# Hybrid decoder block: activation sums and low halves moved from GpSimd to VectorE, eight weight units stored split

## The reference, cut to what matters

```python
mod = silu(c) @ w_ada + b_ada; shift, scale, gate = split(mod, 3)
h = rms_norm(x, norm_g) * (1 + scale) + shift          # (4096, 1024)
proj = h @ w_in                                        # (4096, 3592)
u, z_pool, q, k, v, o, z_mlstm, gates = columns of proj # 512 each, gates 8
pool_out = causal_pool_mixer(u) * silu(z_pool)         # windows 2, 4, 8, 16
q, k = silu(causal_depthwise_conv([q, k]))             # 4 taps
hm = mlstm_chunkwise(q, k, v, ig, log_sigmoid(fg))     # 4 heads of 128, chunks of 128 positions
mlstm_out = rms_norm_per_head(hm) * sigmoid(o) * silu(z_mlstm)
x = x + gate * ([pool_out, mlstm_out] @ w_out)
return rms_norm(x, final_g)
```

## Time and profile before

| What | Value |
| --- | --- |
| Runs, us | 1890.22, 1891.05, 1901.94 |
| Median, us | 1891.05 |
| Profiled execution, us | 1895.02 |
| Its span, first to last instruction, us | 1893.2 |
| Mean granted TensorE clock in it | 0.982 |
| DMA traffic, MB | 368.89 |

### The profile page before, as it was taken

How to read it: one execution, slowest core, us unless ns; L and a number is a source line. 1 busy time by engine, 2 the same in 40 slices (tenths; PEclk the granted TensorE clock), 3 DMA queues, 4 the chain that set the end, 5 groups by cost and what they waited for, 6 DMA issues and landing times.

```text
span 1893.2 us, 25429 instructions
## 1 busy us (share of the span) xinstructions
PE 1759.9 (93%) x8921; PEld 1484.7 (78%) x8921; DVE 1275.2 (67%) x2421; ACT 729.4 (39%) x1692; POOL 633.3 (33%) x491
## 2 busy tenths in 40 slices
PE   6989999989998999988999899998999989998898
PEld 6878879768897788867888678976789768897786
DVE  7786684857748586476855668476684866738583
ACT  4444342443425343343334434244242443424321
POOL 0145235430345204542155402634026430355200
PEclk9999999999999999999999999999999999999999
DMA  9998955468564774657755686446955469554762
GB/s 340 321 330 279 264 148 201 128 175 253 146 212 123 202 249 120 220 131 215 212 154 184 156 244 176 179 134 157 286 149 184 131 166 277 134 205 124 222 185 78
DMA packets 398548, 368.89 MB, mean 195 GB/s; under 512 B 258172, under 2 KB 291924, under 8 KB 397908
## 3 DMA queue, kind: packets, MB, share of 16 engines
q1 hardware_dynamic: 383188, 344.57, 59.8%
q10 hardware_dynamic: 15232, 22.69, 4.5%
HBM read 309.31 MB, written 57.87 MB: 194 GB/s over the span
## 4 chain that ended last, share of the span: by engine, by line
PE 58%; DVE 16%; DMA 11%; SPq 7%; issue 3%; ACT 3%; POOL 0%; ACTq 0%; DVEq 0%; POOLq 0%
PE ps_acc L697 12%; PE ps_acc L699 12%; PE ps_acc L698 12%; SPq L505 5%; DVE sb_hm L2006 4%; DVE sb_acc_cv L2006 4%; DMA sb_w_split<-w_kept 3%; PE ps_num L697 3%; PE ps_num L698 3%; PE ps_num L699 3%; DMA sb_w_raw<-s_kept 3%; DMA hm_kept<-sb_kT 2%; PE ps_kv L697 2%; PE ps_kv L698 2%; PE ps_kv L699 2%
## 5 line engine op out<-in xcount | busy, mean ns | idle before, releaser
L697 PE MATMUL ps_acc<-sb_hT_hi,sb_w_split 128*128 128x512 f32 x1088 | 438.6, 403 | 34.7 <-DMA sb_w_split<-w_kept 25.1
L699 PE MATMUL ps_acc<-sb_hT_hi,sb_w_split 128*128 128x512 f32 x1088 | 429.5, 395 | 0.0
L698 PE MATMUL ps_acc<-sb_hT_lo,sb_w_split 128*128 128x512 f32 x1088 | 428.8, 394 | 0.0
L697 PEld LDWEIGHTS ps_acc<-sb_hT_hi,sb_w_split 128*128 128x128 f32 x1088 | 207.3, 191 | 84.6 <-issue 38.5
L1489 POOL TENSOR_TENSOR sb_w_split<-sb_w_raw,sb_w_split 128x512 fp32r<-128x512 f32 x126 | 178.6, 1431 | 194.7 <-ACT sb_w_split L1059 193.3
L699 PEld LDWEIGHTS ps_acc<-sb_hT_hi,sb_w_split 128*128 128x128 f32 x1088 | 207.4, 191 | 45.5
L698 PEld LDWEIGHTS ps_acc<-sb_hT_lo,sb_w_split 128*128 128x128 f32 x1088 | 207.7, 191 | 40.7
L1542 POOL TENSOR_TENSOR sb_h_rs<-sb_h_var,sb_mhalf 128x4 f32<-128x4 f32 x32 | 33.9, 1060 | 437.5 <-DVE sb_h_var L2104 437.5
L1531 POOL TENSOR_TENSOR sb_t_split<-sb_t_raw,sb_t_split 128x512 fp32r<-128x512 f32 x56 | 90.2, 1645 | 149.5 <-ACT sb_t_split L1065 149.5
L1059 ACT ACTIVATE sb_w_split<-sb_w_raw 128x512 fp32r<-128x512 f32 x196 | 114.8, 625 | 64.2 <-DMA sb_w_raw<-s_kept 55.5
L2006 DVE SCALAR_TENSOR_TENSOR sb_acc_cv<-sb_shifted,sb_par,sb_acc_cv 128x512 f32<-128x512 f32 x96 | 106.6, 1110 | 43.7 <-ACT sb_acc_cv L1313 40.5
(11 more groups left out here) (292 smaller groups left out, 4055.7 us busy)
## 6 DMA issues: line engine op xcount, KB each, us to landing
sb_w_split<-w_kept SPq DMA_DIRECT2D x232, 512.0 KB, 5.6
sb_w_raw<-w_in SPq DMA_DIRECT2D x132, 256.0 KB, 2.8
sb_w_split<-w_kept SPq DMA_DIRECT2D x56, 520.0 KB, 5.1
sb_w_raw<-s_kept SPq DMA_DIRECT2D x112, 256.0 KB, 3.4
sb_x_res<-x SPq DMA_DIRECT2D x34, 512.0 KB, 5.1
out<-sb_qT SPq DMA_DIRECT2D x32, 512.0 KB, 2.9
sb_x_in<-x SPq DMA_DIRECT2D x112, 128.0 KB, 4.0
w_kept<-sb_w_split SPq DMA_DIRECT2D x24, 512.0 KB, 6.8
```

The lines of the kernel that those rows point to most:

```text
L697: pe.matmul(dst, st_hi, mv_hi, start=start, stop=False, skip_group_check=resumed)
L698: pe.matmul(dst, st_hi, mv_lo, start=False, stop=False, skip_group_check=resumed)
L699: return pe.matmul(dst, st_lo, mv_hi, start=False, stop=stop, skip_group_check=resumed)
```

## The change

On VectorE, `sum_t` and `low_t` take the place of GpSimd's, ahead of `gates_read`; ScalarE splits each sum when it is ready, ahead of its copy of v. `ZO_DVE` becomes all units from 8 on, twenty; VectorE's groups of low halves in `zo_late` are cut anew, as are ScalarE's groups. Units 0 to 7 (`ZO_KEPT`) are split as before in block 1, and stored as high and low half by `keep_zo`, each before the load six units on; there the loads of units 8 to 15 also wait for the store of the unit eight before. From block 2 on units 0 to 7 are loaded with `load_w`, 512 KB instead of 256, and no engine splits them. `keep_keys` issues one of its DMAs at each of units 33 to 48. The two `load_x` stand before unit 52 and wait for the end of product 7. In block 0 the sum rounds go to units 26, 31, 36 and 41, their stores to 30, 35, 40 and 45.

```diff
-ZO_DVE = [u for u in range(8, ZO_UNITS) if u % 2 == 0]
+ZO_KEPT = 8
+ZO_RAW = ZO_UNITS - ZO_KEPT
+ZO_DVE = [u for u in range(ZO_KEPT, ZO_UNITS)]
-SUM_ROUNDS = {12 + 8 * r: r for r in range(4)}
-SUM_STORES = {17 + 8 * r: r for r in range(4)}
+SUM_ROUNDS = {26 + 5 * r: r for r in range(4)}
+SUM_STORES = {30 + 5 * r: r for r in range(4)}
...
             def load_zo(b, u):
                 m = QK_END + u
+                if u < ZO_KEPT and b > 1:
+                    load_w(b, m)
+                    return
                 slot_free(b, m)
+                if b == 1 and u in range(8, 8 + ZO_KEPT):
+                    sp.wait_ge(w_kept_done[slot(b, m)], 16 * zo_kept_count(u - 8))
...
+            def keep_zo(u):
+                m = QK_END + u
+                sp.wait_ge(zo_lo_pool, u + 1)
+                sp.dma_start(both(w_kept[m], m), both(w_split[:, slot(1, m), :], m).bitcast(F32)).then_inc(
+                    w_kept_done[slot(1, m)], 16)
...
             def late_block(b, last):
                 for m in range(LOW, UNITS[1]):
+                    if b == 1 and m - 6 - QK_END in range(ZO_KEPT):
+                        keep_zo(m - 6 - QK_END)
+                    if m == TILE_UNITS[1] and not last:
+                        sp.wait_ge(zo_full, zo_no(b, 7, 1))
+                        load_x(b + 1, 0)
+                        load_x(b + 1, 1)
...
-                    if m in (36, 37, 38, 39):
-                        keep_keys(b, m - 36)
+                    if m in range(33, 49):
+                        keep_keys(b, (m - 33) // 4, (m - 33) % 4)
...
-                    if m == 57 and not last:
-                        load_x(b + 1, 0)
-                        load_x(b + 1, 1)
...
-                    pool.wait_ge(acc_full, so_far(TASKS, b))
-                    pool.wait_ge(o_ready, b * NC)
-                    for j in range(2):
-                        sum_t(b, j)
-                    for j in range(2):
-                        low_t(b, j)
                     for u in ZO_POOL:
                         low_zo(b, u)
...
+                def sum_t():
+                    t1, t2, t3, t4 = [[t_raw[:, n, 1, j, :, :] for j in range(2)] for n in range(4)]
...
+                    in_turn()
+                    dve.wait_ge(acc_full, so_far(TASKS, b))
+                    dve.wait_ge(h_lo, b * PREPS + PREPS)
+                    for j in range(2):
+                        token_half(t1[j], 0, 2 + j)
+                        token_half(t3[j], 1, 2 + j)
+                        token_half(t2[j], 0, j)
+                        token_half(t4[j], 1, j)
+                    both_halves(t3, t3, t1, ALU.subtract, 6)
+                    both_halves(t1, t1, t2, ALU.subtract, 9)
+                    both_halves(t2, t3, t2, ALU.add, 11)
+                    both_halves(t4, t4, t2, ALU.subtract, 13)
...
                     did(o_ready, b * NC)
+                    sum_t()
+                    low_t()
                 in_turn()
```

More of the change, by code:

```diff
@@ L378, in kept_count, with zo_kept_count, zo_hi_no @@
             return [n for n in KEPT if slot(0, n) == slot(0, m)].index(m) + 1
+        def zo_kept_count(u):
+            return len([n for n in KEPT if slot(0, n) == slot(1, QK_END + u)]) + 1
+        def zo_hi_no(b, u):
+            return (b - 1) * ZO_RAW + u + 1
         def halves(m):
@@ L1059, in split_zo, with split_t @@
                 act.activation(w_split[:, s, 0:512], w_raw[:, s, 512:1024], ACT.Copy).then_inc(zo_hi_done, 1)
-            def split_t(b, j):
-                act.wait_ge(t_step, 16 * (b - 1) + 8 * (j + 1))
-                for n in (1, 0, 2, 3):
-                    act.activation(t_split[:, n, 0, j, :, :], t_raw[:, n, 1, j, :, :], ACT.Copy).then_inc(t_hi_done, 1)
+            def split_t(b):
+                for i, n in enumerate((2, 0, 1, 3)):
+                    for j in range(2):
+                        act.wait_ge(t_step, 16 * (b - 1) + 8 + 2 * i + j + 1)
+                        act.activation(t_split[:, n, 0, j, :, :], t_raw[:, n, 1, j, :, :], ACT.Copy).then_inc(t_hi_done, 1)
             def square_first(c):
@@ L1187, in one_block @@
                         split_w(m)
+                else:
+                    split_t(b)
                 act.wait_ge(v_done, b + 1)
@@ L1260, in zo_late @@
                     early, after = [oz[:, j, :] for j in range(2)], [oz[:, 2 + j, :] for j in range(2)]
-                    for u in (6, 7):
+                    for u in (6, 7, 8):
                         split_zo(b, u)
@@ L1264, in zo_late @@
                     exponents()
-                    for u in range(8, 12):
+                    for u in range(9, 14):
                         split_zo(b, u)
@@ L1273, in zo_late @@
                         zo_tanh_of(j, zo_tanh_at[j], early[j])
-                    for u in range(12, 16):
+                    for u in range(14, 17):
                         split_zo(b, u)
@@ L1278, in zo_late @@
                     load_inter_row(0)
-                    for u in range(16, 24):
+                    for u in range(17, 25):
                         split_zo(b, u)
                     zo_hold(7, zo_c)
-                    for u in range(24, 28):
+                    for u in range(25, 28):
                         split_zo(b, u)
@@ L1316, in one_block @@
                             split_w(m + 1)
-                        if not first and t in (3, 4):
-                            split_t(b, t - 3)
                         if not first and t >= 5:
@@ L1486, in low_zo @@
             def low_zo(b, u):
-                pool.wait_ge(zo_hi_done, (b - 1) * ZO_UNITS + u + 1)
+                if u < ZO_KEPT and b > 1:
+                    return
+                pool.wait_ge(zo_hi_done, zo_hi_no(b, u))
                 s = slot(b, QK_END + u)
@@ L1843, in low_zo, with token_half, both_halves, low_t @@
                                         ALU.subtract).then_inc(zo_lo_dve, 1)
+                def sum_t():
+                    t1, t2, t3, t4 = [[t_raw[:, n, 1, j, :, :] for j in range(2)] for n in range(4)]
+                    at = 16 * (b - 1)
+                    def token_half(dst, half, c):
+                        ks = slice(4 * half, 4 * half + 4)
+                        V.tensor_tensor(dst, hT_hi[:, ks, chunk(c)].bitcast(F32), hT_lo[:, ks, chunk(c)].bitcast(F32),
+                                        ALU.add).then_inc(t_step, 1)
+                    def both_halves(dst, left, right, op, n):
+                        for j in range(2):
+                            dve.wait_ge(t_step, at + n + j)
+                            V.tensor_tensor(dst[j], left[j], right[j], op).then_inc(t_step, 1)
+                    in_turn()
+                    dve.wait_ge(acc_full, so_far(TASKS, b))
+                    dve.wait_ge(h_lo, b * PREPS + PREPS)
+                    for j in range(2):
+                        token_half(t1[j], 0, 2 + j)
[6 more added lines that the diff above has]
+                    both_halves(t4, t4, t2, ALU.subtract, 13)
+                def low_t():
+                    dve.wait_ge(t_step, 16 * b)
+                    for i, n in enumerate((2, 0, 1, 3)):
+                        for j in range(2):
+                            dve.wait_ge(t_hi_done, 8 * (b - 1) + 2 * i + j + 1)
+                            V.tensor_tensor(t_split[:, n, 1, j, :, :], t_raw[:, n, 1, j, :, :],
+                                            t_split[:, n, 0, j, :, :].bitcast(F32), ALU.subtract).then_inc(t_lo_done, 1)
+                    did(t_lo_done, 8 * b)
                 if first:
@@ L1965, in zo_late @@
                         zo_sum(early[j], zo_z[j], 1 + j)
-                    for u in range(12, 16):
+                    for u in range(12, 14):
                         low_zo(u)
@@ L1969, in zo_late @@
                         zo_mix(early[j], zo_tanh_at[j], early[j], 1 + j, 1 + j)
-                    for u in range(16, 20):
+                    for u in range(14, 21):
                         low_zo(u)
@@ L1976, in zo_late @@
                         zo_sum(after[j], zo_y[j], 3 + j)
-                    for u in range(20, 24):
+                    for u in range(21, 24):
                         low_zo(u)
```

39 lines of the change are left out of this document (8 added, 31 removed).

## The result

The kernel after takes 1794.3 us (median of 4, 1789.6 to 1795.3) against 1893.1 (4 runs, 1890.2 to 1901.9) beside it: ratio 0.9466, 95% interval 0.9429 to 0.9503. The forecast was 1821 us. The direction was right; the gain, 98.8 us, is some 40% larger than the 70 us of the forecast's sum, and 1794.3 lies just under the range's low end of 1797. The profiled execution took 1794.8 us, with a span of 1793.0.

The account below looks back on a forecast made before the run. TensorE, busy 93% of the span, was the bound, so time could come only from its idle stretches and clock. Blocks 2 to 7: 17.0 + 12.5 + 15 + 12.5 + 13 = 70; 1895.0 - 70 = 1825, less 4: 1821 us; range 1797 to 1862.

Parts of the forecast that it names:

- C: TensorE's waits for low halves in products 6, 5 and 7: 22.9 us open in blocks 2 to 7, 15 taken.
- A: TensorE's seven waits of 2.8 us for VectorE's row of maxima, once per late block: 17.0 us to go.
- B: TensorE's waits for GpSimd's low halves in products 1 and 2: 12.5 us to go from block 2 on.
- E: Waits for w_kept weights in the zp tiles, delayed by x issues: 13.7 us in blocks 2 to 7, 12.5 taken.
- D: TensorE's wait for w_kept weights at unit 52, 1.3 us a block, some 7.5 us: expected to stay.
- slower rival: The 24 operations moved to VectorE do not fit V; at 1.75 us each the kernel takes 1971 us; chance 3%.
- The clock: TensorE's drops to its lower clock in blocks 2 to 7: 13 us back, bounds 3 and 15.8.
- Block 0: Closer sum rounds cost +9 us in stalls, query tiles give back perhaps 4; together +5 us, bounds -4 and +14.
- All of it comes back: Every wait of A, B, C and E from block 2 on goes, with the clock: 82 us, 1797 us; chance 15%.
- The transfers stay late: Landing of raw units, not GpSimd, caused C; C stays, with half the clock's loss: 1845 us; chance 20%.
- VectorE is the bound in the products: Low halves stay at 1.35 us, leaving 6 us a block, 36 in all: 1857 us; chance 6%.
- The sum rounds: Rounds of sums in block 0 cost it another 15 us: 1836 us; chance 6%.

Follow-up runs that it names:

- e8: Kernel after with 16 more sums on VectorE within V in each of blocks 1 to 7: ratio to before 0.9716, 50 us slower than after.
- f5: Kernel before with the new order of splits and units 0 to 7 stored split, sums still on GpSimd: ratio 0.9725, 52 us faster than before.
- f1: Kernel before with only the 20 low halves of units 8 to 27 all made by VectorE: ratio to before 1.0002.
- e2: Kernel after with every second of the 20 low halves back on GpSimd: ratio to before 0.9476, 4 us slower than after, within the interval.
- f2: Kernel before with the key stores spread over units 33 to 48 and the new order of splits: ratio 0.9856, 27 us faster than before.
- f6: Kernel before with only the new order of ScalarE's splits and VectorE's low halves: ratio 0.9875, 24 us faster than before.
- g1: Kernel after with the old order of ScalarE's splits and VectorE's low halves: ratio to before 0.9437, nothing lost.
- e3: Kernel after with the key stores again in four groups of four at units 36 to 39: ratio to before 0.9519, 12 us slower than after.
- g3: Kernel after with both the old order of splits and the key stores in groups of four: ratio to before 0.9578, 23 us slower than after.
- e4: Kernel after with activation sums, their low halves and splits on GpSimd and ScalarE as before: ratio to before 0.9621, 32 us slower than after.
- g2: Kernel after with the old order of splits and every second of the 20 low halves on GpSimd: ratio to before 0.9431, nothing lost.
- e1: Kernel after with the next block's x loads issued behind unit 57 again: ratio to before 0.9597, 27 us slower than after.

## Why the forecast came out short

The bounds on TensorE, the four kinds of wait and their places held. Two steps failed. The sum priced a wait at its row and put what it costs beyond that at nothing: 12.8 us. And the term for C was 15 us where 22.9 came, with the wrong cause. The first is what carries the time below the range, whose low end had every listed wait gone. Of the forecast's 70 us for blocks 2 to 7 and the 95 measured:

- **A, B, E: the waits held.** The forecast took 17.0 + 12.5 + 12.5 = 42. In the lists A and B are gone from block 2 on, and E too. It was 13.1, not 13.7 (the forecast put D at 7.5, and it was 8.1); D grew by 0.7, so the w_kept row gave 12.4. The cover for the 24 operations held as well: 17.3 us were expected, 14.7 came, and e8 puts the edge where the slower rival had it, at cover plus slack. What is wrong is how I shared them out: A was not the sums' alone, since f5 halves it.
- **C: 15 taken of 22.9, and the wrong cause.** All of it went. I credited the spread key stores and VectorE's halves, and kept a third back for full DMA engines. The halves are worth nothing (f1, e2). The key stores alone are worth little once the order is new (f2 against f6), and 12 us undone. I had passed over the moved splits; the kernel before with them alone is 24 us faster, and with them in place unit 17 is not late: a hold is left instead of two waits. Either cure keeps C away in the kernel after (g1 loses nothing; e3's 12 us stand at the hold), both gone cost 23 (g3).
- **The clock: 13 taken, 15.5 measured.** The mechanism was right: short waits gone, the clock stays at its upper level (of blocks 2 to 6 four lose nothing to it). The whole loss had been 20.1 us, not the 15.8 that two decimals of six windows gave.
- **What was not in the sum, the larger miss: 12.8 us in neither idle time nor clock.** It is at the waits themselves, and a row shows how. The wait of 2.37 us in g3:

```profile
1040.69 0.39 PE L723 MATMUL ps_num<-sb_w_split,sb_t_split 128*128 128x512 f32 x1
1040.92 0.39 PE L724 MATMUL ps_num<-sb_w_split,sb_t_split 128*128 128x512 f32 x1
1043.68 0.50 PE L722 MATMUL ps_num<-sb_w_split,sb_t_split 128*128 128x512 f32 x1 [2.37 <-DVE sb_w_split L1838]
1044.02 0.45 PE L723 MATMUL ps_num<-sb_w_split,sb_t_split 128*128 128x512 f32 x1
```
  From start to start it is 2.76 us, where the step is 0.23; the loss is 2.53, and the next step takes 0.34 instead of 0.23. So the row of 2.37 stands for 2.64 us: 0.27 more. Blocks 2 to 7 have 54 waits before and 11 after, and 43 x 0.27 = 11.6 of the 12.8 us (an estimate). The other traces bear it out: over blocks 2 to 6 of all runs but e8 (its trace lacks some matmul records), a block's time less idle time and clock loss is 208.1 us and 0.27 for each of its waits, by a fitted line (correlation 0.91).
- Added up: C 7.9, clock 2.5, unlisted 12.8, and 2.2 of shorter waits for ScalarE's tanh (L1108), which the sum did not have: 25.4 against the 25.2 us that were missing.
- **Block 1** was forecast at -5 and came at -6.0, with 4.6 us of new waits behind late units where some 6 were reckoned. **Block 0** was forecast at +5 and came at +1.0: its stalls were there (4.51, 2.06 and 1.33 us, forecast 3.5, 4 and 1.5), but the query tiles gave back nearly all of their 8.3 us, not 4.

*All of it comes back* was the nearest rival, with 82 in blocks 2 to 7: right about the waits, and 13 short by the unlisted part. *The transfers stay late* named C's cause rightly, a raw unit's landing and not GpSimd, and was wrong that the landings would stay: their median rose from 3.4 to 4.2 us, but unit 17's fell to 3.6 to 4.2. *VectorE is the bound in the products* falls with the halves at 0.684 us. (Its price rests on a slip: 38.4 us less 5.3 and 2.8 leaves 30.3, not 32. Another, on which nothing hangs: block 2 took 225.2 us before, not 227 or more.) *The sum rounds* falls with block 0's 1.0 us, *slower* with the 4.06 us that VectorE still waits. The rule of the Trainium skill (SBUF — State Buffer, Who interferes with whom) fits the taps (2.33, and 5.07 beside GpSimd, again in e4), but it was no reason for a gain in the products: with both engines at it, e2 and g2 lost nothing.

## What to carry to other kernels

Undo every part by itself, and put every part in by itself: one that the title names may be worth nothing, and one that looks like bookkeeping a quarter of the gain when put into the old kernel, and still cost nothing when undone in the new one. Where a wait's releaser is the last of a chain (load, split, half), making that last step faster moves nothing as long as the load is what is late; ask also what DMAs the engines in the chain issue between its steps. And a TensorE-bound kernel with many short waits gains more than the list of waits adds up to: here 66.9 us of idle time stood for 95.2.

## What was not expected of the hardware

- A wait of TensorE cost 0.27 us more than its row: 2.64 against 2.37 in g3, and 0.27 a wait over the traces.
- Eight x issues took SyncE 12.96 us (before) and 12.62 (e1) behind unit 57, and 7.46 ahead of unit 52, all three in block 3 or 4. The DMA engines were as busy beside them (0.98, 0.98 and 0.97), so how busy they are doesn't explain it, and no run shows what does.
- Unit 17's transfer of 256 KB took 5.8 to 8.3 us in the three runs where two row loads of 256 KB left within 1.6 us of its issue, and 3.4 to 4.9 in the others.
- On VectorE sums and halves of 128x512 took 0.61 us back to back in V, but 0.72 where each waits for its turn (e8).
- At waits of 4.9 us and more at the log gates the clock was down every time in e8. D's waits in blocks 2 to 7 of the kernel after, up to 1.9 us, never brought it down, but one of 1.87 us did in e8 (lower level at 1080 to 1084 us), and one of 1.97 us for ScalarE in the kernel after (1122 to 1126 us). So a wait's length alone doesn't tell.
